# The unit stage of a hybrid RWKV-7 and attention encoder: TensorE's turn grouped by shape of tile, transposes by heads, both directions' y added in PSUM

## The chip, the core and the metric

One core of a Trainium2 chip runs the whole layer in float32. The metric is the device time of one launch in microseconds; 3246.91 us is the median of three runs of the kernel before (3246.37 to 3249.95).

## What is computed

Two sequences (512 and 2048 tokens, laid end to end: 2560) go through one layer: a projection, an RWKV-7 mixer in both directions, differential attention, and an output stage. The part that the change touches is the recurrence of the mixer, 8 heads of 64 channels:

```python
def step(state, inp):
    r_t, w_t, k_t, v_t, a_t, b_t = inp
    sa = jnp.einsum('dbhij,dbhj->dbhi', state, a_t)
    state = (state * w_t[..., None, :] + sa[..., :, None] * b_t[..., None, :]
             + v_t[..., :, None] * k_t[..., None, :])
    y_t = jnp.einsum('dbhij,dbhj->dbhi', state, r_t)
    return state, y_t
_, ys = lax.scan(step, state0, xs)
y = jnp.moveaxis(ys[:, 0] + ys[::-1, 1], 0, 1)
```

d is the direction (forward, backward); the y of both directions are added at the end.

## The kernel before

The stages follow each other behind barriers: projection and convolution (`conv_phase`), the rest of the projection with the inverses of the small triangular blocks (`rest_phase`), the unit stage (`unit_phase`), the chain of states (`chain_phase`), attention of both sequences, output.

The unit stage takes the recurrence apart into 80 units: 20 chunks of 128 tokens times 4 pairs of heads. A unit loads a pack (`pk`: a, r, b, k, v of both directions, channels on partitions, one head in partitions 0 to 63, the other in 64 to 127) and the inverses of its 64x64 diagonal blocks (`tt`, `tf`). Then TensorE runs seven steps for it (d: direction, h: head):
- `scores` (L1439, L1442): products b.a, b.r, k.a, k.r into four banks `sc[d][h]`, weights of 64 rows and 128 columns; VectorE masks them into `su` (`masked`, L1346).
- `turned` (L1473, L1475, L1479): seven 128x128 transposes of v, a, b, k and a matmul of two columns for the bonus, into the banks of `sc[0]`; ScalarE copies them to `vz`, `ax`, `bn`, `bk_tok` (L1303 to L1308).
- `off_blocks` (L1411) and `joined` (L1423): the corner that joins the two 64x64 inverses, 64x64 tiles in the bank `xq`; VectorE copies after each (`off_block` L1358, `solved` L1352, the latter into `tt`).
- `inner` (L1465): 128x128 weights from `su` against v of 64 columns, into `xq`; VectorE copies it beside a in `ax` (`inner_part`, L1364).
- `applied` (L1453): the inverse `tt` times `ax`, 128x128, into the bank `wb`; ScalarE copies it to `wz` (`joined` of ScalarE, L1294).
- `full_outputs` (L1484, weights 128x128) and `half_outputs` (L1484, weights 128x64): y, the change of the state and its decay into the two banks `ob[h]`. ScalarE's `y_part` (L1288) copies y of one direction, VectorE's `sums` finishes the carries (L1376) and adds y of the other direction (L1379), ScalarE's `own` (L1280) copies the rest, `bonus` (L1313) writes beside them.

A turn of the loop does steps of three units at once. TensorE's order in turn n is `off_blocks(n + 1)`, `joined(n)`, `scores(n + 2)`, `applied(n)`, `inner(n + 1)`, `turned(n + 2)`, `full_outputs(n)`, `half_outputs(n)`. VectorE and ScalarE have a hand-written order of their own, GpSimd prepares the decays (`fp`, `ad`, L1263 to L1270), and SyncE issues, in this order per turn, the pack of unit n + 4, its corner blocks, the solved blocks of n + 3, and the stores of n - 1. Every step waits on semaphores that count units. A float32 matmul leaves two matmul and two weight-load records, a transpose one of each. Some buffers lie in rooms that attention uses later, so the trace calls the third `su` at_kT, the third `vz` and `bk_tok` at_v, and `tt` and two of the packs pack_room; the mask and the identity are corner_room.

Of the kernel before, what the change touches and what calls it, by code (L numbers as in the profile page):

```python
# [1087 lines left out]

class UnitAhead:
# [48 lines left out]
def unit_phase(nc, ahead, sequences, tokens, packs, tblk, nblk, carry, local, kept, ident_d, full, idle, late):  # L1138
# [5 lines left out]
    with Phase(nc, "un") as ph:  # L1144
# [4 lines left out]
        tf = [ph.sb(f"tf{i}", [P, 2, 64]) for i in range(3)]  # L1149
# [6 lines left out]
        fp = [idle.v_room[:, 640 + 2 * i:642 + 2 * i] for i in range(3)]  # L1156
        bn = [idle.v_room[:, 648 + 2 * i:650 + 2 * i] for i in range(3)]
        ad = [ph.sb(f"ad{i}", [P, 2, 192])[:, :, :] for i in range(2)] + [idle.v_room[:, 656:1040].rearrange("p (d n) -> p d n", d=2)]
# [7 lines left out]
        s = {n: ph.sem(n) for n in (  # L1166
            "const", "setup", "tf0", "tf1", "tf2", "fp_ready", "ad_ready", "sc_ready", "su_done", "va_ready", "va_evac", "bk_ready", "bk_evac",
            "bonus_done", "x_ready", "x_evac", "xf_ready", "xf_evac", "q_ready", "q_evac", "wz_ready", "wz_evac",
            "out_ready", "carry_evac", "y_evac", "own_evac", "sum_evac", "carry0", "carry1", "local0", "local1", "local2")}
# [15 lines left out]
        def real(n):  # L1185
            return 0 <= n < NI
# [5 lines left out]

        def halves(h):
            return slice(64 * h, 64 * h + 64), slice(64 - 64 * h, 128 - 64 * h)

        @block.sync
        def _(sp):
            def load_corners(n):
                if n == last_solved:
                    sp.wait_ge(s["stored"], 64 * (NCH // 4))  # L1200
                for i in range(2):
                    sp.dma_start(tf[n % 3][64 * i:64 * i + 64, :, :], ahead.n_v[ahead.lane(n)][i][:, 2 * i:2 * i + 2, :]).then_inc(s[f"tf{n % 3}"], 16)

            def next_pack(n):
                sp.wait_ge(s["ad_ready"], 4 * (n - 3) + 4)
                sp.wait_ge(s["bk_ready"], n - 2)
                ahead.load_pack(sp, n, pk[n % 3][:, :])

            def next_corners(n):
                sp.wait_ge(s["xf_ready"], n - 2)  # L1210
                load_corners(n)

            def store(n):
# [5 lines left out]
                sp.wait_ge(s["sum_evac"], n * 2 + 2)  # L1219
# [4 lines left out]
            for n in range(NI):  # L1224
# [3 lines left out]
                if n + 3 < NI:  # L1228
                    sp.wait_ge(s["wz_ready"], n + 1)
# [5 lines left out]
            sp.wait_ge(s["wz_ready"], last_use + 1)  # L1235
# [9 lines left out]
        def _(pool):  # L1245
# [10 lines left out]
            assert n == 3  # L1256
            pool.wait_ge(s["const"], 32)
            for n in range(NI):
                f, a = fp[n % 3], ad[n % 3]
                if n >= 3:  # L1260
# [1428 lines left out]
```

## Time and profile before

| | |
|---|---|
| median of three runs | 3246.91 us (3246.37 to 3249.95) |
| profiled execution: its time, its span | 3243.25 us, 3241.4 us |
| TensorE busy (matmuls) | 3129.7 us, 97% |
| VectorE, ScalarE, GpSimd busy | 2371.7, 1501.2, 796.3 us |
| unit stage | from about 1319 to 1931 us |
| mean granted TensorE clock | 0.986 of full speed |

Times are microseconds unless ns is written. PE is TensorE's matmuls, PEld its weight loads, which overlap them, DVE is VectorE, ACT ScalarE, POOL GpSimd, SP SyncE. `64*128` behind a tile name is the part of the array that an instruction uses, rows by columns; `x8` counts records. Matmuls are pipelined: the time between two starts tells what one costs, the duration is longer and tells when its result is there.

### The profile page before, as it was taken

How to read it: one execution, taken by the hardware profiler on the slowest of the kernel's cores; microseconds unless marked ns; L12 is line 12 of the kernel's file. 1: busy time of each engine (PE TensorE's matmuls, PEld its weight loads, DVE VectorE, ACT ScalarE, POOL GpSimd, SP SyncE). 2: the span in 40 equal slices, each digit the busy share in tenths (PEclk: the TensorE clock that was granted, in tenths of full speed). 3: DMA queues.
4: the chain of work that ended last, by engine and by line, in shares of the span. 5: the costliest groups of instructions: out<-in, count | busy, mean ns of one | idle time of the engine just before them, and what ended most of it. 6: DMA issues, size and time to landing. Idle time of an engine off the chain costs nothing. (4 is left out here: it accounts for less than half of the span.)

```text
span 3241.4 us, 62850 instructions
## 1 busy us (share of the span) xinstructions
PE 3129.7 (97%) x23985; PEld 2129.7 (66%) x23985; DVE 2371.7 (73%) x4366; ACT 1501.2 (46%) x3649; POOL 796.3 (25%) x987
## 2 busy tenths in 40 slices
PE   8999999999999999899999988899999979999998
PEld 6888787544444444699999977577777744444444
DVE  4676676599999996477777767788888978854544
ACT  4555555344344344344444432577777722213322
POOL 0333343400000000122222210244444422221221
PEclk9999999999999999899999998999999999999999
DMA  4444443822442431655444437400000065531211
GB/s 172 150 137 139 154 150 118 301 80 65 123 119 71 124 103 55 177 171 152 135 133 134 133 99 247 132 18 18 18 18 15 25 250 175 175 120 59 72 74 42
DMA packets 312280, 377.15 MB, mean 116 GB/s; under 512 B 121756, under 2 KB 233832, under 8 KB 309552
## 3 DMA queue, kind: packets, MB, share of 16 engines
q1 hardware_dynamic: 296832, 361.64, 34.7%
q10 hardware_dynamic: 15152, 11.50, 1.1%
q8 instruction: 193, 3.16, 0.4%
q14 instruction: 103, 0.84, 0.1%
HBM read 205.31 MB, written 167.77 MB: 115 GB/s over the span
## 5 line engine op out<-in xcount | busy, mean ns | idle before, releaser
L2067 PE MATMUL at_g<-at_kT,at_qz 64*128 64x512 f32 x1088 | 285.7, 610 | 14.4 <-PEq L44 9.1
L2093 PE MATMUL at_pb<-at_v,at_attT 64*128 64x128 f32 x4352 | 282.7, 277 | 5.7 <-ACT at_o L1951 2.7
L658 PE MATMUL cv_pj<-u_room,w 128*128 128x257 f32 x1248 | 279.6, 383 | 2.0 <-DVEq L491 1.1
L658 PEld LDWEIGHTS cv_pj<-u_room,w 128*128 128x128 f32 x1248 | 236.8, 191 | 46.4 <-issue 12.0
L2093 PEld LDWEIGHTS at_pb<-at_v,at_attT 64*128 64x128 f32 x4352 | 261.4, 188 | 7.6 <-issue 7.2
L1080 PE MATMUL rs_tm<-w,rs_uT 128*128 128x512 f32 x480 | 207.7, 592 | 0.0
L1943 ACT COPY at_attT<-at_tb 128x512 f32<-128x512 f32 (+1 forms) x288 | 146.7, 561 | 108.7 <-PE at_tb L2079 108.7
L1020 DVE TENSOR_TENSOR rs_tmp<-rs_tt,u_room 128x63 f32<-128x63 f32 (+20 forms) x189 | 169.6, 898 | 27.3 <-POOL rs_tt L907 21.7
L1080 PE MATMUL rs_tm<-w,x_pair 128*128 128x512 f32 x416 | 182.6, 599 | 6.8 <-PEq L44 6.8
L658 PE MATMUL cv_pj<-cv_uT,w 128*128 128x257 f32 x832 | 183.5, 379 | 0.0
L1022 DVE TENSOR_TENSOR rs_tt<-rs_tt,rs_tmp 128x63 f32<-128x63 f32 (+20 forms) x189 | 173.2, 917 | 6.5
L658 PEld LDWEIGHTS cv_pj<-cv_uT,w 128*128 128x128 f32 x832 | 156.3, 189 | 26.9 <-issue 4.6
L2067 PEld LDWEIGHTS at_g<-at_kT,at_qz 64*128 64x128 f32 x1088 | 120.5, 191 | 78.5 <-issue 49.7
L1080 PEld LDWEIGHTS rs_tm<-w,rs_uT 128*128 128x128 f32 x480 | 90.4, 190 | 110.0 <-issue 110.0
L2304 ACT COPY fn_ops<-fn_tr 128x512 f32<-128x512 f32 x60 | 35.0, 583 | 248.9 <-PE fn_tr L2514 246.8
L176 POOL TENSOR_TENSOR pack_room<-cv_ak,cv_up 128x512 f32<-128x512 f32 x38 | 52.3, 1375 | 397.1 <-ACT full L390 397.1
L1935 ACT ACTIVATE at_sca<-at_sca,at_nm 128x2048 f32<-128x2048 f32 (+1 forms) x64 | 107.8, 1684 | 89.2 <-DVE at_nm L1997 89.1
L1080 PEld LDWEIGHTS rs_tm<-w,x_pair 128*128 128x128 f32 x416 | 79.2, 192 | 104.4 <-issue 104.4
L2571 PE MATMUL fn_acc<-pack_room,fn_ops 128*128 128x512 f32 x320 | 147.1, 593 | 0.4 <-DVE fn_xh L2441 0.4
L1997 DVE CUSTOM_DVE_ANT_0 at_scb<-at_g,at_wide,at_mx 128x512 f32<-128x512 f32 x192 | 143.1, 745 | 0.0
L2571 PE MATMUL fn_acc<-at_kT,fn_ops 128*128 128x512 f32 x320 | 141.0, 593 | 1.7 <-issue 1.7
L337 ACT COPY cv_win<-cv_pj 128x257 f32<-128x257 f32 x120 | 44.6, 372 | 210.5 <-PE cv_pj L658 210.4
(371 smaller groups left out, 7222.4 us busy)
## 6 DMA issues: line engine op xcount, KB each, us to landing
scratch_packs<-pack_room SPq DMA_DIRECT2D x19, 2048.0 KB, 6.7
pack_room<-scratch_packs SPq DMA_DIRECT2D x54, 640.0 KB, 4.1
un_pk<-scratch_packs SPq DMA_DIRECT2D x25, 640.0 KB, 4.1
w<-in_w_in_dram SPq DMA_DIRECT2D x6, 2048.0 KB, 14.4
scratch_gate<-rs_tok_out SPq DMA_DIRECT2D x40, 256.0 KB, 2.6
scratch_q_kT<-rs_qk_out SPq DMA_DIRECT2D x40, 256.0 KB, 4.5
scratch_local<-un_local_out SPq DMA_DIRECT2D x80, 128.0 KB, 1.9
at_v<-scratch_gate SPq DMA_DIRECT2D x20, 512.0 KB, 5.6
```

What stands on the lines that cost most here:

```text
L176: engine.tensor_tensor(pk_of(k)[:, :, at:at + P], v, e, ALU.mult).then_inc(s[signal], 1)
L337: nc.scalar.copy(dst[0:rows_of(i), HALF * hf:HALF * hf + HALF], pj[n % 3][at:at + rows_of(i), 0:HALF]).then_inc(s["pj_evac"], 1)
L658: last = nc.tensor.matmul(pj[n % 3][0:r, 0:HALF], w[:, c, m * P:m * P + r], uT[b % 2][:, c, HALF * hf:HALF * hf + HALF], start=(c == 0), s ...
L1020: st.step(nc.vector.tensor_tensor(part, column, row, ALU.mult))
L1022: last = nc.vector.tensor_tensor(target, target, part, ALU.add)
L1080: last = nc.tensor.matmul(tm[n % 6][:, :], uT[b % 2][:, k, half], w[:, k, at:at + 512], start=(k == 0), stop=(k == KC - 1))
L1935: nc.scalar.activation(t[:, 0:S], t[:, 0:S], ACT.Exp, bias=nm[:, g % 2, m:m + 1], scale=-1.0, accum_out=rs[:, g % 2, m:m + 1]).then_inc(s[ ...
L1943: nc.scalar.copy(attT[g % 2][:, BR * r:BR * r + BR, half], tb[i][:, 0:64 * BR].rearrange("p (c q) -> p c q", q=64)).then_inc(s["tp_evac"], 1)
L1997: nc.vector.tensor_tensor_reduce(out=scores_of(g, m)[:, at:at + 512], in0=gb[m][:, 512 * i:512 * i + 512], in1=wide[:, away + at:away + at ...
L2067: nc.tensor.matmul(gb[m][:, c * 512:(c + 1) * 512], qz[n % 2][rows, h, :], kT[rows, h, at:at + 512], start=True, stop=True).then_inc(s["sc ...
L2093: last = nc.tensor.matmul(pb[i][:, 0:P], attT[g % 2][rows, c, :], v[rows, c, h * P:(h + 1) * P], start=(c == 0), stop=(c == count - 1))
L2571: last = nc.tensor.matmul(banks(g)[bank][:, :], ops[g % 2][:, a, k, :], rhs[:, k, :], start=(fresh and k == 0), stop=(k == Q - 1), skip_gr ...
```

## The change

TensorE's turn is put in two groups by the shape of the tile. All matmuls with 64 rows and 128 columns come first, those with 128 rows and 64 columns after them: `scores(n + 2, 0)`, `turned(n + 2)`, `scores(n + 2, 1)`, then `applied(n)`, `inner(n + 1)`, `full_outputs(n)`, `joined(n + 1)`, `half_outputs(n)`, `off_blocks(n + 2)`. To that end

- `turned` transposes each head by itself (14 transposes of 64 rows), head 0 into the bank `wb`, head 1 into `xq`, which are written again later in the turn; ScalarE copies each bank's 450 columns in one instruction to a new tile `tk`, in which `inner_part` puts its 256 columns as well;
- `applied`, `inner` and `full_outputs` are split into two column halves of 64;
- `off_blocks` and `joined` use all 128 rows, with zeros in the half that doesn't count: `tf` is twice as wide and cleared once at the start, and GpSimd clears the corner of `tt` for each unit, which `joined` waits for (`tt_clear`);
- y of both directions adds up in `ob[h][.., 0:128]`; VectorE's addition goes;
- `scores` takes a direction as an argument and waits for that direction's masks alone; ScalarE and VectorE follow the new order; a semaphore that two halves raise counts two a unit.

```diff
+TK_V, TK_A, TK_BK, TK_BONUS, TK_ONE = 0, 64, 192, 448, 450
+TK_X = TK_ONE
+TK_HEAD, TK_END = (0, TK_X + 256), 2 * TK_ONE + 256
...
+        tf = [t.rearrange("p (d h c) -> p d h c", d=2, h=2) for t in (idle.q0_room[:, 0:256], idle.q0_room[:, 256:512], ph.sb("tf2", [P, 256])[:, :])]
...
-        vz = [ph.sb(f"vz{i}", [P, P])[:, :] for i in range(2)] + [idle.v_room[:, 512:640]]
-        bk_tok = [ph.sb(f"bk_tok{i}", [P, 2, 2, P])[:, :, :, :] for i in range(2)] + [idle.v_room[:, 0:512].rearrange("p (k d c) -> p k d c", k=2, d=2)]
-        ax = [ph.sb(f"ax{i}", [P, 2, 2, P]) for i in range(2)]
-        xf = [ph.sb(f"xf{i}", [P, 2, 64]) for i in range(2)]
+        tk = [ph.sb(f"tk{i}", [P, TK_END])[:, :] for i in range(2)] + [idle.v_room[:, 0:TK_END]]
+        xf = [idle.v_room[:, 1552 + 128 * i:1680 + 128 * i].rearrange("p (h c) -> p h c", h=2) for i in range(2)]
...
-        tr = sc[0]
...
+        tr = [wb, xq]
...
+            for t in tf:
+                for d in range(2):
+                    setup(nc.gpsimd.memset(t[64 - 64 * d:128 - 64 * d, d, :, :], 0.0))
...
+                    for d in range(2):
+                        nc.gpsimd.memset(tt[n % 3][64 * d:64 * d + 64, 2 * d:2 * d + 2, 64 - 64 * d:128 - 64 * d], 0.0).then_inc(s["tt_clear"], 1)
+                        pool.wait_ge(s["tt_clear"], 2 * (n - 3) + d + 1)
...
-                nc.scalar.copy(vz[n % 3], tr[0][:, 0:P]).then_inc(s["va_evac"], 1)
                 for h in range(2):
-                    nc.scalar.copy(ax[n % 2][:, :, h, 64 * h:64 * h + 64], tr[0][:, P:3 * P].rearrange("p (d c) -> p d c", d=2)[:, :, 64 * h:64 * h + 64]).then_inc(s["va_evac"], 1)
-                nc.scalar.copy(bn[n % 3], tr[0][:, 3 * P:3 * P + 2]).then_inc(s["va_evac"], 1)
-                act.wait_ge(s["bk_ready"], n + 1)
-                nc.scalar.copy(bk_tok[n % 3].rearrange("p k d c -> p (k d c)"), tr[1][:, :]).then_inc(s["bk_evac"], 1)
+                    nc.scalar.copy(tk[n % 3][:, TK_HEAD[h]:TK_HEAD[h] + TK_ONE], tr[h][:, 0:TK_ONE]).then_inc(s["tk_evac"], 1)
...
+                if real(n + 2):
+                    turned(n + 2)
+                if real(n - 1):
                     own(n - 1, 0)
+                    own(n - 1, 1)
                 if real(n):
                     joined(n)
-                if real(n - 1):
-                    own(n - 1, 1)
-                    bonus(n - 1)
-                if real(n + 2):
-                    turned(n + 2)
+                    bonus(n)
...
-                dve.wait_ge(s["y_evac"], n * 2 + h + 1)
-                nc.vector.tensor_tensor(local_out[n % 3][ys, 0, :], ob[h][ys, 192:192 + P], local_out[n % 3][ys, 0, :], ALU.add).then_inc(s["sum_evac"], 1)
...
+                if real(n + 1):
+                    off_block(n + 1)
                 if real(n - 1):
                     sums(n - 1, 0)
-                if real(n):
-                    solved(n)
-                if real(n + 1):
-                    off_block(n + 1)
+                    sums(n - 1, 1)
                 if real(n + 2):
                     masked(n + 2, 0)
-                if real(n - 1):
-                    sums(n - 1, 1)
-                if real(n + 2):
                     masked(n + 2, 1)
                 if real(n + 1):
                     inner_part(n + 1)
+                    solved(n + 1)
...
+                    hs, ys = halves(h)
+                    mm(tr[h][:, TK_BONUS:TK_BONUS + 2], p_[hs, PK_RKK:PK_RKK + P], pair[hs, :], start=True, stop=True)
+                blocks = [PK_V] + [PK_AR + 256 * d + P * A_SLOT[d] for d in range(2)] + [PK_BK + 256 * (k % 2) + P * (k // 2) for k in range(4)]
+                for k, at in enumerate(blocks):
                     for h in range(2):
                         hs, ys = halves(h)
...
+                        last = nc.tensor.transpose(tr[h][:, 64 * k:64 * k + 64], p_[hs, at:at + P], ident[hs, hs])
+                        if k == 6:
+                            last.then_inc(s["tk_ready"], 1)
...
-                pe.wait_ge(s["va_evac"], 4 * n + 3)
+                pe.wait_ge(s["tk_evac"], 2 * min(n + 2, NI - 1) + 1)
...
-                        last = mm(wb[:, P * u:P * u + P], tt[n % 3][:, u, :], ax[n % 2][:, d, h, :], start=True, stop=True)
-                last.then_inc(s["wz_ready"], 1)
+                        for c in range(2):
+                            cs = slice(64 * c, 64 * c + 64)
+                            last = mm(wb[cs, P * u:P * u + P], tt[n % 3][:, u, cs], ax_of(n, d, h), start=True, stop=True)
+                            if u == 3:
+                                last.then_inc(s["wz_ready"], 1)
...
+                        last = mm(xq[e, 256 + 64 * h:320 + 64 * h], su[n % 3][:, d, h, SU_OFF[d]:SU_OFF[d] + 64], tf[n % 3][:, d, h, :], start=True, stop=True)
+                        if h == 1:
+                            last.then_inc(s["xf_ready"], 1)
...
-                        last = mm(xq[:, 128 * d + 64 * h:128 * d + 64 * h + 64], su[n % 3][:, d, h, SU_AK[d]:SU_AK[d] + P], vz[n % 3][:, 64 * h:64 * h + 64], start=True, stop=True)
-                last.then_inc(s["x_ready"], 1)
...
-                p_ = pk[n % 3]
...
-                mm(tr[0][:, 384:386], p_[:, PK_RKK:PK_RKK + P], pair[:, :], start=True, stop=True)
-                for k, at in enumerate([PK_V] + [PK_AR + 256 * d + P * A_SLOT[d] for d in range(2)]):
-                    last = nc.tensor.transpose(tr[0][:, k * P:(k + 1) * P], p_[:, at:at + P], ident[:, :])
-                last.then_inc(s["va_ready"], 1)
-                for k in range(4):
...
+                        for c in range(2):
+                            cs = slice(64 * c, 64 * c + 64)
+                            last = mm(xq[cs, 128 * h + 64 * d:128 * h + 64 * d + 64], su[n % 3][:, d, h, SU_AK[d] + 64 * c:SU_AK[d] + 64 * c + 64], v_of(n, h), start=True, stop=True)
+                            if d == 1 and h == 1:
+                                last.then_inc(s["x_ready"], 1)
...
+                        r, e = slice(64 * d, 64 * d + 64), slice(64 - 64 * d, 128 - 64 * d)
+                        last = mm(xq[r, 384 + 64 * h:448 + 64 * h], xf[n % 2][:, h, :], tt[n % 3][:, 2 * d + h, e], start=True, stop=True)
+                        if h == 1:
+                            last.then_inc(s["q_ready"], 1)
...
-                        into(ob[h][:, 192 * d:192 * d + P], wz[n % 2][:, d, h, :], su[n % 3][:, d, h, SU_RB[d]:SU_RB[d] + P], d == 0)
+                        hs, ys = halves(h)
+                        rb = su[n % 3][:, d, h, SU_RB[d]:SU_RB[d] + P]
+                        into(ob[h][hs, 192 * d:192 * d + P], wz[n % 2][:, d, h, hs], rb, d == 0)
+                        into(ob[h][ys, 0:P], wz[n % 2][:, d, h, ys], rb, d == 0)
...
-                        into(ob[h][own[1 - h], 192 * d:192 * d + P], V[h], su[n % 3][:, d, h, SU_RK[d]:SU_RK[d] + P])
+                        into(ob[h][own[1 - h], 0:P], V[h], su[n % 3][:, d, h, SU_RK[d]:SU_RK[d] + P])
...
-                        last = into(ob[h][own[h], 192 * d + P:192 * d + 192], w[:, d, h, own[h]], bk[:, 0, d, own[h]])
-                last.then_inc(s["out_ready"], 1)
+                        last = into(ob[h][own[h], 192 * d + P:192 * d + 192], w[:, d, h, own[h]], bk_of(n, 0, d, h))
+                        if d == 1:
+                            last.then_inc(s["out_ready"], 1)
...
             for n in turns:
-                if real(n + 1):
-                    off_blocks(n + 1)
-                if real(n):
-                    joined(n)
                 if real(n + 2):
-                    scores(n + 2)
+                    scores(n + 2, 0)
+                    turned(n + 2)
+                    scores(n + 2, 1)
                 if real(n):
                     applied(n)
                 if real(n + 1):
                     inner(n + 1)
-                if real(n + 2):
-                    turned(n + 2)
                 if real(n):
                     full_outputs(n)
+                if real(n + 1):
+                    joined(n + 1)
+                if real(n):
                     half_outputs(n)
+                if real(n + 2):
+                    off_blocks(n + 2)
```

## Rows read from the trace of the kernel before

**Rows 1.** Busy time from 1340 to 1920, then clock, DMA share, GB/s: PE, PEld, DVE, ACT, POOL.

```profile
1340.00:1920.00 580.00, 578.49 (x7558) 529.43 (x7558) 426.70 (x1089) 263.21 (x937) 155.38 (x462) 1.00 0.46 139
```

**Rows 2.** TensorE in order of time, one turn: start, duration, line, tiles, shapes, count.

```profile
1603.41 0.45 PE L1411 MATMUL un_xq<-un_tf,un_su 64*64 64x64 f32 x8
1603.69 0.40 PE L1423 MATMUL un_xq<-pack_room,un_xf 64*64 64x64 f32 x8
1604.03 0.60 PE L1439 MATMUL un_sc<-un_pk 64*128 64x192 f32 x4
1604.45 0.60 PE L1442 MATMUL un_sc<-un_pk 64*128 64x256 f32 x4
1604.89 0.49 PE L1439 MATMUL un_sc<-un_pk 64*128 64x192 f32 x4
1605.21 0.60 PE L1442 MATMUL un_sc<-un_pk 64*128 64x256 f32 x4
1605.74 1.16 PE L1453 MATMUL un_wb<-un_ax,pack_room 128*128 128x128 f32 x8
1606.73 1.00 PE L1465 MATMUL un_xq<-un_vz,un_su 128*128 128x64 f32 x8
1607.57 0.34 PE L1473 MATMUL un_sc<-un_pair,un_pk 128*128 128x2 f32 x2
1607.77 0.53 PE L1475 MATMUL un_sc<-corner_room,un_pk 128*128 128x128 f32 x3
1608.13 0.60 PE L1479 MATMUL un_sc<-corner_room,un_pk 128*128 128x128 f32 x4
1608.57 1.06 PE L1484 MATMUL un_ob<-un_su,un_wz 128*128 128x128 f32 x8
1609.56 0.45 PE L1484 MATMUL un_ob<-un_vz,un_bk_tok 128*64 128x64 f32 x8
1609.84 0.61 PE L1484 MATMUL un_ob<-un_su,un_vz 128*64 128x128 f32 x8
1610.28 0.28 PE L1484 MATMUL un_ob<-un_wz,un_bk_tok 128*64 128x64 f32 x4
...
1610.62 0.29 PE L1484 MATMUL un_ob<-un_bk_tok,un_wz 128*64 128x64 f32 x4
1610.84 0.45 PE L1411 MATMUL un_xq<-un_tf,at_kT 64*64 64x64 f32 x8
```

**Rows 3.** By tile: durations in ns, least, median, most; first and last start.

```profile
L1465 PEld LDWEIGHTS un_xq<-un_vz,un_su x432: 192/192/333, 1331.4 to 1918.9; 128*128 128x128 f32 x144
```

**Rows 4.** TensorE in attention, in order of time.

```profile
2302.57 0.69 PE L2079 MATMUL at_tb<-ident,at_sca 64*128 64x64 f32 x16
2303.06 2.04 PE L2093 MATMUL at_pb<-at_v,at_attT 64*128 64x128 f32 x32
2304.90 0.63 PE L2067 MATMUL at_g<-at_kT,at_qz 64*128 64x512 f32 x2
```

**Rows 5.** Groups of ScalarE and VectorE, 1340 to 1920 us: shapes, count, busy, mean ns, idle before.

```profile
L1294 ACT COPY un_wz<-un_wb 128x512 f32<-128x512 f32 x79 | 46.3, 586 | 188.4 <-PE un_wb L1453 188.4
...
L1308 ACT COPY un_bk_tok<-un_sc 128x512 f32<-128x512 f32 x52 | 32.7, 629 | 0.0
...
L1280 ACT COPY kept<-un_ob 64x128 f32<-64x128 f32 x116 | 30.2, 260 | 15.9 <-DVE kept L1376 13.1
...
L1379 DVE TENSOR_TENSOR un_local_out<-un_ob,un_local_out 64x128 f32<-64x128 f32 x156 | 45.1, 289 | 4.9
```

**Rows 6.** All engines in the last turn, in order of time.

```profile
1923.74 1.16 PE L1453 MATMUL un_wb<-un_ax,pack_room 128*128 128x128 f32 x8 [1.43 <-DVE pack_room L1352]
...
1924.94 0.59 ACT L1294 COPY un_wz<-un_wb 128x512 f32<-128x512 f32 x1 [1.92 <-PE un_wb L1453]
1925.55 0.26 ACT L1280 COPY kept<-un_ob 64x128 f32<-64x128 f32 x1
...
1926.06 0.97 PEld L1484 LDWEIGHTS un_ob<-un_su,un_wz 128*128 128x128 f32 x8 [1.35 <-ACT un_wz L1294]
```

More of the change, by code:

```diff
@@ L1400, in _, with turned @@
             mm = nc.tensor.matmul
-            def off_blocks(n):
-                pe.wait_ge(s["su_done"], 4 * n + 4)
-                pe.wait_ge(s[f"tf{n % 3}"], n // 3 * 32 + 32)
+            def turned(n):
+                p_ = pk[n % 3]
+                if n == 0:
+                    pe.wait_ge(s["setup"], 9)
+                if n:
+                    pe.wait_ge(s["tk_evac"], 2 * n)
+                if n >= 3:
+                    pe.wait_ge(s["wz_evac"], n - 2)
                 if n:
                     pe.wait_ge(s["xf_evac"], n)
-                    pe.wait_ge(s["x_evac"], n)
+                if n >= 2:
+                    pe.wait_ge(s["x_evac"], n - 1)
+                    pe.wait_ge(s["q_evac"], 2 * (n - 1))
@@ L1440, in scores @@
-                    for h in range(2):
-                        hs, ys = halves(h)
-                        mm(sc[d][h][:, 0:256], p_[hs, b_at + P:b_at + 256], p_[hs, ar:ar + 256], start=True, stop=True).then_inc(s["sc_ready"], 1)
+                        last = nc.tensor.transpose(tr[h][:, 64 * k:64 * k + 64], p_[hs, at:at + P], ident[hs, hs])
+                        if k == 6:
+                            last.then_inc(s["tk_ready"], 1)
+            def scores(n, d):
+                p_ = pk[n % 3]
+                ar = PK_AR + 256 * d
+                off = ar + 64 if d == 0 else ar
+                b_at = PK_BK + 256 * d
+                if d == 0:
+                    pe.wait_ge(s[f"in{n % 3}"], n // 3 * 16 + 16)
+                if n:
+                    pe.wait_ge(s["su_done"], 4 * (n - 1) + 2 * d + 2)
+                for h in range(2):
+                    hs, ys = halves(h)
+                    mm(sc[d][h][:, 256:448], p_[hs, b_at:b_at + P], p_[hs, off:off + 192], start=True, stop=True)
+                for h in range(2):
+                    hs, ys = halves(h)
+                    mm(sc[d][h][:, 0:256], p_[hs, b_at + P:b_at + 256], p_[hs, ar:ar + 256], start=True, stop=True).then_inc(s["sc_ready"], 1)
@@ new lines, in off_blocks @@
+            def off_blocks(n):
+                pe.wait_ge(s["su_done"], 4 * n + 4)
+                pe.wait_ge(s[f"tf{n % 3}"], n // 3 * 32 + 32)
+                pe.wait_ge(s["tk_evac"], 2 * n + 2)
+                if n:
+                    pe.wait_ge(s["x_evac"], n)
+                    pe.wait_ge(s["q_evac"], 2 * n)
+                for h in range(2):
+                    for d in range(2):
+                        e = slice(64 - 64 * d, 128 - 64 * d)
+                        last = mm(xq[e, 256 + 64 * h:320 + 64 * h], su[n % 3][:, d, h, SU_OFF[d]:SU_OFF[d] + 64], tf[n % 3][:, d, h, :], start=True, stop=True)
+                        if h == 1:
+                            last.then_inc(s["xf_ready"], 1)
@@ new lines, in joined @@
+            def joined(n):
+                pe.wait_ge(s["xf_evac"], n + 1)
+                pe.wait_ge(s["x_evac"], n + 1)
+                pe.wait_ge(s[f"st{n % 3}"], n // 3 * 32 + 32)
+                if n >= 3:
+                    pe.wait_ge(s["tt_clear"], 2 * (n - 2))
+                for h in range(2):
+                    for d in range(2):
+                        r, e = slice(64 * d, 64 * d + 64), slice(64 - 64 * d, 128 - 64 * d)
+                        last = mm(xq[r, 384 + 64 * h:448 + 64 * h], xf[n % 2][:, h, :], tt[n % 3][:, 2 * d + h, e], start=True, stop=True)
+                        if h == 1:
+                            last.then_inc(s["q_ready"], 1)
@@ L1496, in half_outputs @@
             def half_outputs(n):
                 own = [slice(64 * h, 64 * h + 64) for h in range(2)]
-                V = [vz[n % 3][:, 64 * h:64 * h + 64] for h in range(2)]
-                bk, w = bk_tok[n % 3], wz[n % 2]
-                pe.wait_ge(s["bk_evac"], n + 1)
+                V = [v_of(n, h) for h in range(2)]
+                w = wz[n % 2]
                 for d in range(2):
                     for h in range(2):
-                        into(ob[h][own[h], 384 + 64 * d:448 + 64 * d], bk[:, 1, d, own[h]], V[h])
+                        into(ob[h][own[h], 384 + 64 * d:448 + 64 * d], bk_of(n, 1, d, h), V[h])
```

122 lines of the change are left out of this document (47 added, 75 removed).

## The prediction

> **What bounds the kernel now.** I read the page's busy times (TensorE 97% of the span), then the busy time by stage, then one turn of the unit stage in order of time. In the unit stage (from 1340 to 1920 us, [rows 1]) TensorE is 578.49 of 580 us busy at a granted clock of 1.00, VectorE 427, ScalarE 263, GpSimd 155. So the stage has one bound, TensorE, and every nanosecond that TensorE saves counts until one of its waits is no longer covered. The stages follow each other behind a barrier, so a shorter unit stage shortens the whole by as much.
>
> [rows 2] are one whole turn in steady state: L1411 starts at 1603.41 and again at 1610.84, so a turn takes 7.43 us, with 80 units of which 78 or so run at this pace. An engine that looks full can still be badly used, so I read starts, not durations: the difference between the starts of two groups is what a group costs the array. Four facts come out.
> - Column pairs work. From 1610.28 to 1610.62 lie three groups of 4 records of 128x64, two column halves in turn: 0.34 us for 6 pairs, 0.058 for a pair of records side by side. With 128 moving columns a pair costs 0.11 us (1609.84 to 1610.28 for 8 records).
> - `inner` (L1465) sends 64 columns past 128x128 weights and takes 0.84 us for 8 records, 0.105 each, though 64 columns need 0.058: it waits for weight loads (192 ns, [rows 3]).
> - The seven transposes of `turned` take 0.36 + 0.44 us, 0.11 each, and its small matmul 0.20.
> - Between shapes something is lost. L1423 has 8 records of 64x64 in 0.34 where 0.234 would do, L1439 takes 0.42 behind the change of shape and 0.32 without one, L1442 0.53 against 0.44, L1453 0.99 for 8 x 0.11, L1484's first group 0.99 for 8 x 0.11, its second 0.28 for 0.23, its last 0.22 for 0.12, and L1411 0.28 for 0.23. Each switch drains the array (0.09 to 0.10) and starts with uncovered weight loads (0.05 into 64 columns, 0.10 into 128): about 0.15, 0.20, 0.20 and 0.15, 0.69 us for the four of a turn.
>
> **The change, part by part, per turn.**
>
> Switches. Four become two: 64x128 to 128x64 and back. Neither pair stands in the trace, but the cost looks like drain plus first load, which gives 0.15 + 0.20. Bounds: the two cheapest kinds (0.30) and the two dearest (0.40). Saved: 0.69 - 0.35 = 0.34 us.
>
> `inner`. 8 records of 128x128 become 16 of 128x64 in 8 pairs of 0.058: 0.47 instead of 0.84. Saved 0.37.
>
> `applied` and `full_outputs`. 16 records in 8 pairs of 0.11 are 0.88, as the 8 of 0.11 were. Nothing. This needs the two column halves to run side by side although both now write one bank, which no 128x64 group does today; but the 64x64 groups L1411 and L1423 write both halves of the bank xq and still do 8 records in 4 pairs of 0.06 to 0.07 [rows 2]. `full_outputs` takes the halves in the order 0, 1, 1, 0; today's groups meet the same half twice only at their borders, at no cost (1609.84, 1610.28).
>
> `turned`. The 14 transposes of 64 rows, two heads side by side, are exactly what attention does at L2079: 16 of them from 2302.57 to 2303.06 [rows 4], 0.49 for 8 pairs, 0.061 each. Seven pairs: 0.43 instead of 0.80. The upper bound is 0.11 a pair (today's transposes, if the loads of 128 columns set the pace). The small matmuls double but go in pairs: 0.20 as today. The first real matmuls behind transposes are late: L2093 takes 1.84 for 16 pairs of 0.11, some 0.05 too much. So 0.20 + 0.43 + 0.05 = 0.68 against 1.00: saved 0.32 (0 at the upper bound).
>
> `joined`, `off_blocks`, `half_outputs`. The same records as pairs of 128x64: nothing.
>
> Sum of TensorE: 7.43 - 0.34 - 0.37 - 0.32 = 6.40 us a turn.
>
> A new wait. `full_outputs(n)` needs `wz`, which ScalarE copies out of `wb` after `applied(n)`. Between the two TensorE has today `inner` and `turned`, 0.84 + 1.00 = 1.84 us. Afterwards only `inner`, 0.47. Counted from the start of the last record of `applied`: it runs 0.275 (in [rows 2] `applied`'s records end at 1605.74 + 1.16 = 1606.90, and the last starts 0.11 before 1606.73), ScalarE starts 0.04 later ([rows 6]: records end at 1923.74 + 1.16 = 1924.90, the copy begins at 1924.94), the copy takes 0.586 [rows 5], the release some 0.05, and the first weight load behind a stall isn't covered, 0.05 to 0.08: 1.02. Its cover is 0.11 + 0.47 = 0.58. Stall 0.44 us a turn, in a place where today there is none (one such wait of 1.35 us is to be seen in the very last turn [rows 6], where the cover is missing as well). Bounds: 0.38, and 0.65 if the release costs 0.25 as it did there (own copy ends 1925.55 + 0.26, next load at 1926.06, with three waits left to pass). Queued behind it on TensorE are `joined(n + 1)`, `half_outputs(n)` and `off_blocks(n + 2)`; `inner_part` and `sums` on VectorE and `y_part` on ScalarE move with them, so it is paid in full.
>
> The other waits, laid out from the start S of `scores(n + 2, 0)`: the transposes end at S + 1.67, ScalarE's first copy of 450 columns takes about 0.53 (between 0.260 for 128 and 0.586 for 512 columns; 0.58 by the slower 0.629 of L1308 [rows 5]) and frees `wb` near S + 2.31; `applied` comes at S + 2.34. That is covered by 0.03 us only, so 0 with an upper bound of 0.1. The second copy (S + 2.85) is wanted by `inner` at S + 3.2: covered by 0.35. ScalarE's `own` copies fit in before `applied` has ended, and its whole turn is about 0.52 + 1.07 + 0.52 + 0.59 + 0.59 = 3.3 us. VectorE works 427/580 x 7.43 = 5.5 us a turn [rows 1] and loses two additions of 0.29 (L1379 [rows 5]): 4.9 of 6.8. In its new order `inner_part` stands behind all but itself and `solved`, about 4.3 us from S + 0.1 and the handovers, near S + 4.6; `joined` wants it at S + 5.1, and `off_blocks` wants `solved`, done near S + 6.2, at S + 6.5. GpSimd gains two clears of 64x128 at the head of its loop behind `wz_ready` of n - 3, which is older than the `carry_evac` that it waits for anyway, and it is busy 155 of 580 us [rows 1]. On SyncE, the corner loads wait for `off_blocks`, now at the end of the turn before and not at the head of this one, the same moment; packs, solved blocks and stores are queued behind it in the same order, and each is wanted over a turn later. DMA is at 0.46 of its time and goes to 0.50.
>
> Per turn: 6.40 + 0.44 = 6.84, saved 0.59; with 78 turns 46 us. At both ends: the six new clears in the setup lie beside the DMAs that ScalarE issues until its first copy; in the last turns the small gains come without a new wait, and the last `sums` ends without two additions. I take 2 us more, bounds 0 and 4. In all 48 us: the profiled execution, 3243.25 us with a span of 3241.4, would become 3195; it lies 3.7 below the median of the runs, so the median goes to 3246.9 - 48 = 3199 us.
>
> **Rivals.**
> (a) The ring of evacuations waits for more than `wz`. The 0.03 us of cover ahead of `applied` is thin, and the transposes may go at 0.11 a pair. For it: two of ScalarE's copies now stand between TensorE's groups. Against: rows for each piece. Price: 0.1 more before `applied`, 0.2 more at `wz` and half of the transposes' upper bound (0.16) leave 0.13 to 0.2 saved: 12 us, 3235 at worst, 3222 in the middle. The Trainium skill (TensorEngine Tiling (Array Packing), PSUM Bottleneck) says that tiling speeds up TensorE but not the evacuation of PSUM, which may then bound; the rows on `wz` say the same of one copy of four, not of the whole.
> (b) The stall at `wz` doesn't come, since the loads behind it are let through or the copy starts earlier. Then 1.03 x 78 + 2: 82 us, 3165. Against: a matmul can't start before its weights are in SBUF, and the sum is made of measured pieces.
> (c) Slower: column halves don't run side by side where they now stand in one bank and take turns. The place is `applied`, `inner` and `full_outputs`. Then 16 records of 0.11, 16 of 0.058 and 16 of 0.11 cost 1.76 + 0.93 + 1.76 instead of 0.88 + 0.47 + 0.88: 2.22 more; the stall at `wz` vanishes (0.93 of cover). 6.40 + 2.22 = 8.62, 1.19 more than today, 93 us: 3340. It decides when more than a quarter of the overlap in these three is lost (0.59 of 2.22). For it: no 128x64 group writes one bank today. Against: L1411 and L1423 in [rows 2], and L1484's column pairs. The rule of the Trainium skill (TensorE: Matmul & The Clock Gate, part 3, what overlaps and what doesn't) that weight loads overlap running matmuls only when they go to another group of rows would mean this, too, since both halves use all rows. The trace disagrees: the column pairs of L1484 go at 0.058 [rows 2], load and matmul together.
> (d) No change: savings and new waits cancel within 6 us. That needs 0.5 us more of stall a turn than I find anywhere.
>
> **How the numbers follow.** The forecast has a chance of 0.76, (a) 0.09, (b) 0.05, (c) 0.06, (d) 0.04. The forecast's own terms: switches -0.05 to +0.05, stall -0.06 to +0.21, `applied` 0 to 0.1, transposes up to +0.32 (unlikely), ends 2 us either way: without the transposes, 3188 to 3229 at the outer ends, most of it below 3215. The range that leaves out 2 in 10 runs from 3176, two thirds of the way to (b), to 3220, into (a). A difference of 0.2% (6.5 us) is about what a measurement of this kernel can tell from none. Faster: 0.76 + 0.09 + 0.05, with a little of (a) given to no change, 0.89; same 0.04; slower 0.07.
>
> **What would show it.** In the profile after: a turn of 6.8 us between starts of L1439's first group; two changes of shape a turn; the fourteen transposes in 0.43; `inner` in 0.47; TensorE idle before `full_outputs` by 0.4 us, released by ScalarE's copy of `wz`; no idle time before `applied`; VectorE's additions gone. If `applied`, `inner` or `full_outputs` take nearly twice what I give them, (c) holds; if idle time stands before `applied` or `joined`, (a). I am wrong altogether if the granted clock in the stage falls from 1.00, for which no row speaks.

## The result, and the profile after

The changed kernel takes 3201.51 us in the median of 4 runs (3199.17 to 3202.11), the kernel before 3246.64 (3243.55 to 3249.95) beside it: a ratio of 0.9855, 95% interval 0.9843 to 0.9867. That is 45.1 us less, where 48 were forecast. The profiled execution took 3202.11 us with a span of 3200.4, so 41.1 and 41.0 below the profiled execution of before.

The first line of the page's busy times (engine, busy us, share of the span, instructions):

```profile
PE 3072.2 (96%) x26625; PEld 2072.3 (65%) x26625; DVE 2323.3 (73%) x4206; ACT 1469.0 (46%) x3409; POOL 829.3 (26%) x1147
```

Over the unit stage, the view of [rows 1]: busy time of PE, PEld, DVE, ACT, POOL, then granted clock, DMA share, GB/s:

```profile
1340.00:1870.00 530.00, 508.83 (x9980) 461.04 (x9976) 373.47 (x919) 227.34 (x689) 184.57 (x610) 1.00 0.52 153
```

TensorE was busy in 578.49 of 580 us [rows 1], now in 508.83 of 530: the stage was bound by TensorE's work and is now bound in part by TensorE's waits. The waits view of TensorE's weight loads, 1340 to 1880 us (engine, tile and line, releaser: us in all, times, longest), says where:

```profile
PEld un_wb L1466 <- issue: 33.1, 77, 0.6
PEld un_ob L1510 <- ACT un_wz L1315: 29.4, 79, 1.6
```

One ordinary turn of TensorE in order of time, the view of [rows 2] (start, duration, line, tiles, shapes, count, idle before and its releaser). `scores` is L1450 and L1453, `turned` L1430 and L1435 (the transposes are left out but for the first), `applied` L1466, `inner` L1491, `joined` L1504, both output parts L1510, `off_blocks` L1480:

```profile
1633.99 0.59 PE L1450 MATMUL un_sc<-pack_room 64*128 64x192 f32 x4
1634.42 0.60 PE L1453 MATMUL un_sc<-pack_room 64*128 64x256 f32 x4
1634.85 0.16 PE L1430 MATMUL un_wb<-un_pair,pack_room 64*128 64x2 f32 x1
...
1634.99 0.25 PE L1435 MATMUL un_wb<-corner_room,pack_room 64*128 64x64 f32 x1
...
1635.45 0.55 PE L1450 MATMUL un_sc<-pack_room 64*128 64x192 f32 x4
1635.83 0.61 PE L1453 MATMUL un_sc<-pack_room 64*128 64x256 f32 x4
1636.47 1.09 PE L1466 MATMUL un_wb<-un_tk,pack_room 128*64 128x128 f32 x16
1637.37 0.66 PE L1491 MATMUL un_xq<-at_v,at_kT 128*64 128x64 f32 x16
1638.25 1.09 PE L1510 MATMUL un_ob<-un_su,un_wz 128*64 128x128 f32 x16 [0.22 <-ACT un_wz L1315]
1639.18 0.40 PE L1504 MATMUL un_xq<-pack_room,at_v 128*64 128x64 f32 x8
1639.41 0.40 PE L1510 MATMUL un_ob<-un_tk 128*64 128x64 f32 x8
1639.64 0.61 PE L1510 MATMUL un_ob<-un_su,un_tk 128*64 128x128 f32 x8
...
1640.54 0.40 PE L1480 MATMUL un_xq<-at_qz,un_su 128*64 128x64 f32 x8
1640.88 0.43 PE L1450 MATMUL un_sc<-pack_room 64*128 64x192 f32 x2
```

The turn is 6.89 us (1633.99 to 1640.88), where it was 7.43 [rows 2]. 14 of the 76 turns behind the third are longer, up to 7.07; their mean is 6.913, before 7.427. So 0.513 a turn and 39.0 us in these 76; the first three turns are 1.0 shorter, and from the last start of L1450 to the next stage 22.1 us pass, where it was 26.3. With a start that is 0.6 us later, the next stage begins 43.6 us earlier (1891.2 for 1934.8). 2.6 of these are lost behind it, in code that isn't changed; I did not follow them, since medians and profiled executions differ by as much.

ScalarE's and TensorE's weight-load rows of the same turn, for the two places where TensorE waits:

```profile
1635.68 0.54 ACT L1323 COPY un_tk<-un_wb 128x450 f32<-128x450 f32 x1 [1.24 <-PE un_xq L1435]
1636.11 0.54 ACT L1323 COPY un_tk<-un_xq 128x450 f32<-128x450 f32 x1
...
1637.61 0.59 ACT L1315 COPY un_wz<-un_wb 128x512 f32<-128x512 f32 x1 [0.53 <-PE un_wb L1466]
```

```profile
1636.44 0.88 PEld L1466 LDWEIGHTS un_wb<-un_tk,pack_room 128*64 128x64 f32 x16 [0.41 <-issue]
...
1638.25 0.85 PEld L1510 LDWEIGHTS un_ob<-un_su,un_wz 128*64 128x64 f32 x16 [0.36 <-ACT un_wz L1315]
```

The copy of `wz` ends at 1638.20, and the next load stands at 1638.25: the forecast stall. The other load, of `applied`, also begins late (1636.44), but its releaser is "issue", nothing that the profile shows: the copy it needs began at 1635.68, and the next began on the same engine at 1636.11, 0.1 before the first one's recorded end; so it was through by 1636.22 at the latest. The load comes 0.22 behind it; 0.11 of that is on the path: the array is free at 1636.36 (1635.83, 0.44 of records, 0.09 until it has run empty), and the first matmul starts at 1636.47. The first experiments are about this place.

### The profile page after: what moved, and what is told of

It is laid out like the page before. It is cut to its first block and busy times, and to the rows that moved or that the text cites. A ratio compares the mean times of both kernels' runs of the same rounds, so it can differ in the third digit from the quotient of the medians.

```text
span 3200.4 us, 67961 instructions
## 1 busy us (share of the span) xinstructions
PE 3072.2 (96%) x26625; PEld 2072.3 (65%) x26625; DVE 2323.3 (73%) x4206; ACT 1469.0 (46%) x3409; POOL 829.3 (26%) x1147
```

## The experiments

All times stand beside runs of the kernel before on the same chip, with medians of 3247.7 to 3248.3 us. The runs go by the first part of their labels (e1, e10 and so on). "Turn" is the distance between starts of the first group of `scores`, in steady state.

**The wait ahead of `applied`.** Theory: the copy is on time, but the list of waits is passed one by one behind it. The edit only reorders the list.

```diff
             def applied(n):
+                pe.wait_ge(s["tk_evac"], 2 * min(n + 2, NI - 1) + 1)
                 pe.wait_ge(s["q_evac"], 2 * n + 2)
                 pe.wait_ge(s["x_evac"], n + 1)
-                pe.wait_ge(s["tk_evac"], 2 * min(n + 2, NI - 1) + 1)
```

> One part of the change altered: in TensorE's step applied, the wait for ScalarE's copy out of wb (tk_evac) stands first in the program and not third; nothing else. In the changed kernel's trace the copy ends 2.23 us after the turn's start, TensorE passes the wait at 2.27, but its first weight load of applied follows at 2.45 (in most turns) to 2.63 us, after two further waits on things that were ready long before; the array would be free at 2.38. Theory: the 0.07 to 0.26 us lost there are the waits that stand behind the late one, not the copy. With the late wait last in TensorE's own order they vanish: a turn of 6.81 to 6.83 us instead of a mean of 6.91, no long turns of 6.98 to 7.07, 7 us less in all, 3194 to 3196 us. Rival: it is the copy itself (the prediction's rival (a)): no change, 3201 to 3202 us, long turns as before.

Measured: 3193.36 us (3191.51 to 3193.69), ratio 0.9826 (0.9808 to 0.9843), and every turn 6.80 to 6.81. The turn in its trace:

```profile
1599.66 0.60 PE L1453 MATMUL un_sc<-pack_room 64*128 64x256 f32 x4
1600.19 1.09 PE L1466 MATMUL un_wb<-at_v,pack_room 128*64 128x128 f32 x16
```

L1453 to L1466 is 0.53, 0.44 of records and 0.09 of drain, where the changed kernel has 0.64 (1635.83 to 1636.47). The program forbids and allows exactly the same, so the order of the list alone costs 8 us (76 turns of 6.913 against 6.807). The first three turns of the profiled execution were 2.1 us longer than the changed kernel's; I did not follow that.

Two more kernels ask what in the order costs: three added waits that are satisfied long before, behind the late one; and the late wait as the last of the list.

```diff
                 pe.wait_ge(s["tk_evac"], 2 * min(n + 2, NI - 1) + 1)
                 if n:
                     pe.wait_ge(s["wz_evac"], n)
+                pe.wait_ge(s["su_done"], 4 * n + 4)
+                pe.wait_ge(s["xf_evac"], n + 1)
+                pe.wait_ge(s["tk_evac"], 2 * n + 2)
```

> The changed kernel with three more waits at the end of applied's list, behind the wait for ScalarE's copy, each for something that happened long before (masked products, off-block copy, copies of the unit itself). They forbid nothing that isn't forbidden already. Theory (satisfied waits behind a late one are passed one after the other, before the first weight load can go, some 0.05 to 0.11 us for each wait instruction): applied starts 0.1 to 0.25 us later than in the changed kernel, a turn of 7.0 to 7.15, 3209 to 3221 us. Rival (the 0.11 us ahead of applied is the copy's own lateness, and waits that are satisfied cost nothing): 3199 to 3203 us.

```diff
                 pe.wait_ge(s["x_evac"], n + 1)
-                pe.wait_ge(s["tk_evac"], 2 * min(n + 2, NI - 1) + 1)
                 if n:
                     pe.wait_ge(s["wz_evac"], n)
+                pe.wait_ge(s["tk_evac"], 2 * min(n + 2, NI - 1) + 1)
```

> The changed kernel with the wait for wz moved ahead of the wait for ScalarE's copy in applied, so that the late wait is the last of the list (in e1 it is the first). Theory (what costs is what must still be passed behind the late wait; the one that rides on the first weight load remains): applied starts 0.03 to 0.1 us earlier, about half of what e1 gained, 3195 to 3199 us. Rival (only the first place of the list is cheap): as the changed kernel, 3200 to 3203 us.

Measured: with three more waits 3199.36 us (3198.22 to 3200.16), ratio 0.9851 (0.9836 to 0.9865), a turn of 6.84, which is not longer than in the changed kernel but 0.05 shorter. With the late wait last 3193.39 (3192.99 to 3195.49), ratio 0.9832 (0.9816 to 0.9848), 6.805: all of e1's gain and not half of it. Both numbers miss the theory as I had put it, and that of the three added waits lies in the rival's range (waits that are satisfied cost nothing). So the times alone don't decide; TensorE's wait records in the traces do, and show what it had wrong (ns from the start of a turn; a wait instruction holds one or two waits, and one more rides on the first weight load):

```
changed kernel:    wait with the late one 2270, a second wait 2381, load 2456, first matmul 2487
  in a long turn:  wait with the late one 2271, a second wait 2557, first matmul 2664
three more waits:  wait with the late one passed at 2273, a second 2328, load 2404
late wait last:    wait with the late one 2270, load 2373
late wait first:   (the late one rides on the load), load 2373
```

The list is packed into instructions, two waits in one, and the place of a wait in the program decides which one it falls into. What costs is each wait *instruction* left behind the late one: 0.055 to 0.11 us, though it is satisfied, and 0.20 to 0.29 in 9 of the changed kernel's 76 turns. With at most the load behind it, the array's own readiness (2374) decides, and nothing is lost. The three added waits happened to be packed so that the late one shared an instruction that was begun earlier. So the mechanism holds, and counting waits, as I did, is the wrong way to price it. Why a satisfied wait takes up to 0.29 in some turns isn't settled. Nor are the 4 turns of 6.95 that e11 still has: they lose 0.09 and 0.05 around `off_blocks`, and 5 of the changed kernel's 14 long turns lose about as much there.

The long turns do have a period. Counted from 0, e11's are turns 24, 40, 56 and 72, and ten of the changed kernel's 14 are the turns 8, 24, 40, 56 and 72 and the turn behind each (e8's stand there too): 16 apart. TensorE's queue leaves 272 records a turn (matmuls, weight loads and waits), and the queue q8, "instruction" in the profile, moves 68 blocks of 16 KB in the 64 turns from 8 on. That is 256 records a block, so a block's border comes back to the same place of a turn after 16 turns. With three more waits a turn has 273 records, and five of its seven long turns stand 15 apart (8, 23, 38, 53, 68), as 256 and 273 would have it. That points to the borders between blocks of TensorE's instructions, but it isn't shown: no run moves a border on purpose, some long turns lie outside the period, and e1, with 272 records too, has no long turn at all.

**The stall at `wz`.** The eight matmuls of `half_outputs` that need only `v` are moved ahead of `full_outputs`, as a cover of 0.67 us:

```diff
+            def v_outputs(n):
...
+                        into(ob[h][own[h], 384 + 64 * d:448 + 64 * d], bk_of(n, 1, d, h), v_of(n, h), d == 0)
...
+                        into(ob[h][own[1 - h], 0:P], v_of(n, h), su[n % 3][:, d, h, SU_RK[d]:SU_RK[d] + P], d == 0)
...
                 if real(n):
+                    v_outputs(n)
                     full_outputs(n)
```

> The eight matmuls of half_outputs that need only v, k and su (0.67 us by the changed kernel's trace) are moved ahead of full_outputs, between inner and it. Theory: full_outputs waits 0.41 us a turn for ScalarE's copy of wz, because only inner (0.47 us) lies between; with 1.14 us of cover the wait is gone and nothing else becomes late: a turn of 6.50 us on average, 32 us less, about 3170 us. Rival 1: the stall only moves, to joined (which wants VectorE's copy of inner's result) or to applied: less than 10 us gained, 3192 or more. Rival 2: the loss before full_outputs is no wait but the array's own (a slower start of the column halves in one bank): no change, 3201 us.

Measured: 3213.97 us (3212.16 to 3215.11), ratio 0.989 (0.9875 to 0.9905), a turn of 7.01: the stall at `wz` is gone, and the kernel is 12 us slower for it. From its turn:

```profile
1610.93 1.07 PE L1510 MATMUL un_ob<-at_kT,un_wz 128*64 128x128 f32 x16
1611.81 0.43 PE L1504 MATMUL un_xq<-pack_room,at_v 128*64 128x64 f32 x8
...
1612.39 0.31 PE L1510 MATMUL un_ob<-at_v,un_wz 128*64 128x64 f32 x4
1613.04 0.45 PE L1480 MATMUL un_xq<-at_qz,un_su 128*64 128x64 f32 x8 [0.34 <-DVE pack_room L1370]
```

`full_outputs` has no idle time ahead of it, but `off_blocks` waits for VectorE's copy of the solved block, which follows on `joined`. The V matmuls had been *that* copy's cover; the matmuls between `joined` and `off_blocks` had shrunk from 1.13 us to 0.46. One cover can't lie at two places. With e1's order as well:

> Both edits of the two runs above together. Theory: both losses are independent waits, so the gains add: a turn of 6.41 us, about 3162 us (39 us below the changed kernel). Rival: with one wait gone the other engines' ring (VectorE: 5 us of work a turn in a fixed order) sets the turn: 3170 us or more.

Measured: 3205.67 us (3204.16 to 3207.19), ratio 0.9865 (0.985 to 0.988), a turn of 6.92. Still slower than the changed kernel.

**What a change of shape costs.** First from the changed kernel, with `joined` set back to 64x64 in its place between 128x64 groups:

```diff
-                        last = mm(xq[r, 384 + 64 * h:448 + 64 * h], xf[n % 2][:, h, :], tt[n % 3][:, 2 * d + h, e], start=True, stop=True)
+                        last = mm(xq[r, 384 + 64 * h:448 + 64 * h], xf[n % 2][e, h, :], tt[n % 3][e, 2 * d + h, e], start=True, stop=True)
```

> One part undone: joined runs as 64x64 tiles again, in its new place between steps of 128x64, so that a turn has four changes of shape and not two; same count of matmuls, same waits, same data. Theory: a change of shape costs a drained array (0.09 to 0.10 us) and uncovered first weights (0.05 us), so 0.29 us a turn, 23 us: 3224 us. Rival: changes of shape cost nothing by themselves and what the kernel before lost at its four borders were waits: 3201 us.

Measured: 3225.66 us (3224.17 to 3228.08), ratio 0.9927 (0.9911 to 0.9943), a turn of 7.19, 0.30 more for two changes of shape; not one record more.

```profile
1618.08 1.09 PE L1510 MATMUL un_ob<-at_kT,un_wz 128*64 128x128 f32 x16 [0.22 <-ACT un_wz L1315]
1619.10 0.45 PE L1504 MATMUL un_xq<-pack_room,at_v 64*64 64x64 f32 x8
1619.48 0.45 PE L1510 MATMUL un_ob<-at_v 128*64 128x64 f32 x8
1619.76 0.61 PE L1510 MATMUL un_ob<-at_kT,at_v 128*64 128x128 f32 x8
```

The same eight records of L1504 take 0.38 to the next group, where they took 0.23; L1510 before them 1.02 for 0.93, and behind them 0.28 for 0.23.

Then from the kernel before, with one part of the change alone. `inner` in column halves:

```diff
-                        last = mm(xq[:, 128 * d + 64 * h:128 * d + 64 * h + 64], su[n % 3][:, d, h, SU_AK[d]:SU_AK[d] + P], vz[n % 3][:, 64 * h:64 * h + 64], start=True, stop=True)
+                        for c in range(2):
+                            cs = slice(64 * c, 64 * c + 64)
+                            last = mm(xq[cs, 128 * d + 64 * h:128 * d + 64 * h + 64], su[n % 3][:, d, h, SU_AK[d] + 64 * c:SU_AK[d] + 64 * c + 64], vz[n % 3][:, 64 * h:64 * h + 64], start=True, stop=True)
```

> The kernel before with one part of the change: the small inner products of inner as 16 records of 128x64 in column pairs, where they were 8 of 128x128. Around them 128x128 groups stay. Theory (a group costs its records and its two borders): records 0.84 -> 0.47, saved 0.37 a turn, but two borders between shapes appear where there was none, one into 64 moving columns (about 0.15) and one into the small matmul of turned (0.15 to 0.20), 0.30 to 0.35 together: a turn of 7.38 to 7.43, 3241 to 3247 us, that is no change that can be measured. Rival (only the records count; borders are dear only at 64x64): 7.06 a turn, 3217 us.

And the transposes by heads:

```diff
-                for k, at in enumerate([PK_V] + [PK_AR + 256 * d + P * A_SLOT[d] for d in range(2)]):
-                    last = nc.tensor.transpose(tr[0][:, k * P:(k + 1) * P], p_[:, at:at + P], ident[:, :])
+                for k, at in enumerate(blocks):
+                    for h in range(2):
+                        hs, ys = halves(h)
+                        last = nc.tensor.transpose(tr[h][:, 64 * k:64 * k + 64], p_[hs, at:at + P], ident[hs, hs])
```

> The kernel before with another part alone: the seven transposes of turned by heads, 14 of 64x128 in row pairs, into the two banks of sc[0], and the evacuation by ScalarE in 8 copies where there were 5. Theory: turned 1.00 -> 0.60, saved 0.40 a turn; two new borders (128x128 to 64x128 and back), 0.15 plus 0.20: 7.38 to 7.43 a turn, 3241 to 3248 us, no change that can be measured; ScalarE's three more copies lie beside TensorE. Rival (records alone count): 7.03 a turn, 3216 us. Second rival (ScalarE's longer row of copies holds up scores, which want the same banks): over 7.45 a turn, slower than 3250 us.

Measured: `inner` alone 3242.71 us (3235.34 to 3245.43), ratio 0.9986 (0.9977 to 0.9995), a turn of 7.344, a little under the theory's 7.38. Heads alone 3248.89 us (3245.54 to 3251.72), ratio 1.0004 (0.9994 to 1.0013), a turn of 7.435. Rows of the first, then of the second:

```profile
1615.91 1.16 PE L1453 MATMUL un_wb<-un_ax,pack_room 128*128 128x128 f32 x8
1616.99 0.69 PE L1467 MATMUL un_xq<-un_vz,un_su 128*64 128x64 f32 x16
1617.61 0.38 PE L1476 MATMUL un_sc<-un_pair,pack_room 128*128 128x2 f32 x2
```

```profile
1629.54 0.63 PE L1480 MATMUL un_sc<-corner_room,pack_room 64*128 64x64 f32 x14
1630.10 1.16 PE L1486 MATMUL un_ob<-at_kT,un_wz 128*128 128x128 f32 x8
1631.19 0.45 PE L1486 MATMUL un_ob<-at_v 128*64 128x64 f32 x8
```

The first saves 0.38 in `inner`'s records and pays 0.30 at its two borders (`applied` 1.08 for 0.99, `inner` 0.62 although its records take 0.46, the small matmul 0.05 more). The second saves 0.39 in `turned` and pays 0.40 (0.09 in `inner`, 0.10 each in the small matmul, the transposes and L1486). In the changed kernel the same two parts bring their 0.38 and 0.39 in full, as no border is added. Either part by itself is worth 0.08 us a turn or nothing.

**y summed in PSUM.** The changed kernel with the two directions of y apart again, and VectorE's additions back:

```diff
+                dve.wait_ge(s["y_evac"], n * 2 + h + 1)
+                nc.vector.tensor_tensor(local_out[n % 3][ys, 0, :], ob[h][ys, 192:192 + P], local_out[n % 3][ys, 0, :], ALU.add).then_inc(s["sum_evac"], 1)
...
-                        into(ob[h][ys, 0:P], wz[n % 2][:, d, h, ys], rb, d == 0)
+                        into(ob[h][ys, 192 * d:192 * d + P], wz[n % 2][:, d, h, ys], rb, d == 0)
```

> The changed kernel with one part undone: y of the two directions is not added up in PSUM but kept in two places of the bank, and VectorE adds them with two additions of 0.29 us a unit, as before the change. TensorE's records are the same in number and shape. Theory of the prediction (VectorE is covered: 4.9 of 6.9 us a turn): no change, 3199 to 3205 us. Rival (VectorE's later half of the turn is near the path: inner_part or solved comes 0.58 us later and joined or off_blocks waits for it): up to 0.3 us a turn more, 3215 to 3225 us.

Measured: 3201.6 us (3200.38 to 3203.28), ratio 0.9863 (0.9848 to 0.9878): the same as the changed kernel. This third part of the change brings no time; VectorE has room.

**A version from these results.** e1's order, and in `joined` and `off_blocks` too the wait that comes last stands first; the V matmuls first, for `wz`; and `full_outputs` parted by direction with `joined` between its parts, so that the solved copy has half of `full_outputs` as its cover in place of the V matmuls.

```diff
                 if real(n):
-                    full_outputs(n)
+                    v_outputs(n)
+                    full_outputs(n, 0)
                 if real(n + 1):
                     joined(n + 1)
                 if real(n):
+                    full_outputs(n, 1)
                     half_outputs(n)
```

> The changed kernel with the cheaper order of waits of e1, the eight matmuls of half_outputs that need only v moved ahead of full_outputs, and full_outputs parted by direction with joined(n + 1) between its two parts, so that the copies of wz and of the solved block are both covered. The waits that come last stand first. Theory (each stall is a copy's length less its cover): the 0.41 at wz shrinks to 0 to 0.1, off_blocks no longer waits for solved (joined is back 0.5 us earlier), applied waits for nothing: records 6.30 to 6.40 plus some 0.1, a turn of 6.40 to 6.50, 3161 to 3170 us. Rival (VectorE's inner_part, done near 4.6 us behind the start of the turn, now releases joined, or solved is late again): 6.6 to 6.9 a turn, 3177 to 3200 us.

Measured: 3166.03 us (3163.93 to 3167.31), ratio 0.9754 (0.9738 to 0.977), a turn of 6.395. Its busy times over 1340 to 1840 us:

```profile
1340.00:1840.00 500.00, 498.51 (x10132) 463.33 (x10129) 374.55 (x933) 231.59 (x702) 186.61 (x616) 1.00 0.56 162
```

TensorE is full again (498.51 of 500), with no idle time between its groups in an ordinary turn; five turns are longer, one of them 7.18, and the mean is 6.421. This is 35 us below the changed kernel. Of the 0.49 us a turn, 0.46 are the stall at `wz` with its uncovered load and 0.08 the order of waits; 0.05 are lost again at the border of `off_blocks`. So what the change does to TensorE's own work is worth some 81 us, and its new waits took 35 of them.

## Why the prediction was right, and where it wasn't

**The work on TensorE.** Forecast 6.40 us a turn without any wait. The changed kernel with e1's order takes 6.805, 0.46 of it the stall: 6.35. The 0.05 between them are mainly the small matmuls, 0.14 for my 0.20. The rest is near the forecast: the transposes 0.46 and 0.05 behind them (0.43 and 0.05), `inner`'s records 0.47 (0.47), `applied` and `full_outputs` 0.88 each of records (0.88), the two switches 0.09 and 0.05, 0.10 and 0.10 (together 0.34 for my 0.35). Rival (c) is out: 16 records of 128x64 that write both halves of one bank go at 0.11 a pair, as the 128x128 records did one by one. So the rule of the Trainium skill (TensorE: Matmul & The Clock Gate, part 3), by which such weight loads wait for the running matmuls, doesn't describe these groups: the trace disagrees. Rival (b) is out as well, since the stall at `wz` came.

**The switches by themselves.** I had read 0.15 to 0.20 each off differences of starts in one trace. e4 gives 0.15, e5 0.15, e6 0.20, each as a mean of two. Right.

**The stall at `wz`.** Forecast 0.44 with its uncovered load (0.38 to 0.65), measured 0.46 (L1491 to L1510 0.88, less 0.47 of records, and 0.05 in L1510). The chain was right link by link: copy 0.586, 0.05 from its end to the load. The Trainium skill (TensorEngine Tiling (Array Packing), PSUM Bottleneck), which I had weighed in rival (a), says that tiling speeds up TensorE but not the evacuation of PSUM. Here the trace agrees in a narrow form only: one copy of four sets the pace, the engine as a whole is busy 227 of 530 us. What I had not asked is which other copy would be late once this stall is gone (e2).

**The wait ahead of `applied`.** This term of the sum failed. I had 0 with a bound of 0.1, worked out from the copy's end, and the copy was even a little earlier than I had it. It cost 0.11 ahead of `applied` in an ordinary turn and 0.20 to 0.29 in nine, on the mean 0.11 a turn (6.913 against e1's 6.807). What the step left out is what TensorE's queue does between the release and the load: one more wait instruction stands between the late one and the load. The list of waits stands in the code, and [rows 6] priced it: 0.25 us from the end of ScalarE's own copy to the next load, with three waits left to pass. I put that into the bound of the stall at `wz`, where in the new kernel the late wait rides on the load and the release took 0.05, and not into the bound of `applied`. Rival (a)'s price ahead of `applied` came true by a mechanism that it doesn't name, and its other two parts didn't.

**The ends.** Forecast 2 us (0 to 4) beside 78 turns, so 3.2 (1.2 to 5.2) beside the 76 that I count here; measured 5.2, the upper bound. I had looked for small gains only. In the last turn `applied` used to wait 1.43 us for VectorE's solved copy [rows 6], as nothing stood between `joined` and it; in the new order the output matmuls do. The turn before it waited as well. Against that the waits ahead of `full_outputs` in these two turns grew, from 0.32 and 1.19 to 1.42 and 1.68 us, so of the 4.2 us at the end only 1.0 is idle time saved (before, then after):

```profile
1917.21 1.16 PE L1453 MATMUL un_wb<-un_ax,pack_room 128*128 128x128 f32 x8 [1.19 <-DVE pack_room L1352]
```

```profile
1878.81 1.09 PE L1510 MATMUL un_ob<-un_su,un_wz 128*64 128x128 f32 x16 [1.42 <-ACT un_wz L1315]
...
1883.83 1.10 PE L1510 MATMUL un_ob<-un_su,un_wz 128*64 128x128 f32 x16 [1.68 <-ACT un_wz L1315]
```

The row of [rows 6] was before me, and I read that view for `wz` alone. The rest I did not take apart.

**The sum.** A turn of 6.913 for my 6.84 is 5.8 us too little saved in 76 turns; 2.0 more than forecast at the ends; a start 0.6 us later; so 43.6 for 48 at the end of the stage. That the median comes to 45.1 of 48 is in part luck: TensorE's work came out 0.05 a turn shorter than forecast and the ends 2.0 us better, against the 0.11 ahead of `applied` and 0.02 more of stall.

**VectorE.** Forecast 4.9 us a turn; 373.47 of 530 us are 4.87 of 6.91. Its sums aren't on the path (e8), as forecast.

## What to carry to other kernels

Price a matmul shape with its neighbours: halving an operation in a mode of its own can gain 0.39 and pay 0.40 at the borders, and the same edit pays in full once its neighbours share the mode. When a group of work is moved or shortened, list for every copy and load what covers it before and after, also of those that had no wait; and put a cover where two copies are both served, or part a group in two. In a list of waits, put the one that comes last where no wait instruction is left behind it, and confirm it in the trace.

## What the hardware showed that I had not expected

A satisfied wait instruction behind a late one took 0.055 to 0.11 us on TensorE, in nine turns of the changed kernel 0.20 to 0.29, and the order of a list of waits was worth 8 us of 3200. Four small matmuls of 64x128 with two moving columns took 0.14 us, where two of 128x128 had taken 0.20 [rows 2]. Most of the long turns stood 16 apart with 272 records a turn (the changed kernel, e8, e11) and 15 apart with 273 (e10), as the borders between blocks of 256 instructions do. e1 has no such turn, and the cause is open.
